# Opening of a two-block forward pass: two of the modulation loads get their own places, x and the small parameters change their turn, and ScalarE's copies change order

## The reference, cut to what matters

```python
def first_block(x, c, ada_w, ada_b, ...):
    cond = jax.nn.silu(c)
    for l in range(DEPTH):                                 # DEPTH = 2
        mod = (cond @ ada_w[l] + ada_b[l])[:, None, :]     # 1024 -> 6 * 1024
        sh_m, sc_m, g_m, sh_f, sc_f, g_f = jnp.split(mod, 6, axis=-1)
        h = x * (1.0 + sc_m) + sh_m
        y = even_mixer(h, ...) if l % 2 == 0 else odd_mixer(h, ...)
        x = layer_norm(DN_ALPHA * x + (1.0 + g_m) * y, ...)
        h = x * (1.0 + sc_f) + sh_f
        y = conv_ffn(h, ...)
        x = layer_norm(DN_ALPHA * x + (1.0 + g_f) * y, ...)
    return x
```

## Time and profile before

| | us |
|---|---|
| median of 3 runs (lowest, highest) | 1171.13 (1169.72, 1172.15) |
| the profiled execution, its own time | 1172.54 |
| its span from the first to the last instruction | 1170.7 |
| granted TensorE clock over the span | 0.989 |
| TensorE busy | 1120.4 |
| GpSimd busy | 832.1 |
| ScalarE busy | 590.6 |
| VectorE busy | 538.4 |

### The profile page before, as it was taken

How to read it: one execution, slowest core, us unless ns; L and a number is a source line. 1 busy time by engine, 2 the same in 40 slices (tenths; PEclk the granted TensorE clock), 3 DMA queues, 4 the chain that set the end, 5 groups by cost and what they waited for, 6 DMA issues and landing times.

```text
span 1170.7 us, 21670 instructions
## 1 busy us (share of the span) xinstructions
PE 1120.4 (96%) x8115; PEld 1026.8 (88%) x8115; DVE 538.4 (46%) x1120; ACT 590.6 (50%) x894; POOL 832.1 (71%) x297
## 2 busy tenths in 40 slices
PE   5899999999999989999999989999999999999997
PEld 2799898999998978899999878999999988999996
DVE  4668877865567675683232551342211333111112
ACT  0455535454544564455454445465876543545444
POOL 3567569988786545898878647556566776988884
PEclk9999999999999999899999999999999999999999
DMA  9987798999986536697566326344444544666562
GB/s 344 318 269 203 247 296 270 339 332 321 300 294 210 143 110 202 182 297 215 182 185 191 110 71 180 109 144 144 139 117 158 183 151 139 208 186 190 184 181 88
DMA packets 253484, 238.03 MB, mean 203 GB/s; under 512 B 18075, under 2 KB 216528, under 8 KB 253424
## 3 DMA queue, kind: packets, MB, share of 16 engines
q1 hardware_dynamic: 235104, 198.70, 55.4%
q10 hardware_dynamic: 17712, 38.28, 9.1%
q0 software_dynamic: 608, 0.22, 0.1%
HBM read 236.12 MB, written 1.05 MB: 203 GB/s over the span
## 4 chain that ended last, share of the span: by engine, by line
PE 68%; DMA 8%; POOL 7%; DVE 6%; ACT 6%; issue 3%; SPq 1%; ACTq 0%; POOLq 0%; DVEq 0%
PE bank L1287 17%; PE bank L1288 16%; PE bank L1289 16%; POOL unit_lo L733 6%; ACT unit_hi L849 3%; PE bank L1321 2%; PE bank L1312 2%; PE bank L1313 2%; DMA raw<-in_ffn_w_up 2%; DMA raw<-in_ev_w_in 2%; DMA ada<-in_ada_w 1%; PE bank L1425 1%; DVE x L2044 1%; PE bank L1528 1%; DMA accg<-in_ada_w 1%
## 5 line engine op out<-in xcount | busy, mean ns | idle before, releaser
L733 POOL TENSOR_TENSOR unit_lo<-raw,unit_hi 128x2048 fp32r<-128x2048 f32 (+5 forms) x87 | 343.7, 3955 | 216.8 <-ACT unit_hi L849 215.8
L1287 PE MATMUL bank<-h_hi,unit_hi 128*128 128x256 f32 x1152 | 327.0, 284 | 0.0
L1288 PE MATMUL bank<-h_lo,unit_hi 128*128 128x256 f32 x1152 | 325.9, 283 | 0.0
L1289 PE MATMUL bank<-h_hi,unit_lo 128*128 128x256 f32 x1152 | 325.9, 283 | 0.0
L784 POOL TENSOR_TENSOR unit_lo<-raw,unit_hi 128x2048 fp32r<-128x2048 f32 (+1 forms) x70 | 257.1, 3672 | 77.3 <-ACT unit_hi L998 65.6
L1287 PEld LDWEIGHTS bank<-h_hi,unit_hi 128*128 128x128 f32 x1152 | 220.7, 192 | 5.3 <-issue 2.5
L1288 PEld LDWEIGHTS bank<-h_lo,unit_hi 128*128 128x128 f32 x1152 | 220.7, 192 | 2.5
L1289 PEld LDWEIGHTS bank<-h_hi,unit_lo 128*128 128x128 f32 x1152 | 220.7, 192 | 0.0
L849 ACT ACTIVATE unit_hi<-raw 128x2048 fp32r<-128x2048 f32 (+5 forms) x97 | 161.2, 1663 | 101.5 <-PE bank L1289 30.3
L787 POOL TENSOR_TENSOR down<-raw_down,down 128x1024 fp32r<-128x1024 f32 x70 | 176.1, 2516 | 0.0
L2177 DVE SCALAR_TENSOR_TENSOR work<-bank,cols,work 128x254 f32<-128x254 f32 (+1 forms) x176 | 72.6, 474 | 131.7 <-ACT work L985 131.7
(11 more groups left out here) (363 smaller groups left out, 2173.3 us busy)
## 6 DMA issues: line engine op xcount, KB each, us to landing
raw<-in_ffn_w_up SPq DMA_DIRECT2D x86, 512.0 KB, 5.2
raw<-in_w_in SPq DMA_DIRECT2D x60, 512.0 KB, 4.7
raw_down<-in_ffn_w_down SPq DMA_DIRECT2D x44, 512.0 KB, 5.4
ada<-in_ada_w ACTq DMA_DIRECT2D x16, 1024.0 KB, 6.9
raw<-in_w_up SPq DMA_DIRECT2D x64, 256.0 KB, 3.0
raw_down<-in_w_down SPq DMA_DIRECT2D x32, 512.0 KB, 3.5
raw<-in_ev_w_in SPq DMA_DIRECT2D x28, 512.0 KB, 5.3
att<-in_ada_w ACTq DMA_DIRECT2D x14, 1024.0 KB, 7.7
```

What stands on the lines that cost most here:

```text
L733: nc.gpsimd.tensor_tensor(ul[g % 2][:, w], raw_home(g)[:, w], uh[g % 2][:, w].bitcast(F32), ALU.subtract).then_inc(lo_up, 1)
L1287: nc.tensor.matmul(o, sh, mh, start=first, stop=False)
L1288: nc.tensor.matmul(o, sh, ml, start=False, stop=False)
L1289: return nc.tensor.matmul(o, sl, mh, start=False, stop=last)
```

## The change

Four things change, all in the opening.

Half 3 of the late modulation (e = 2) gets a place of its own, columns 1024 to 3071 of `work`, and half 4 (e = 3) the two tiles `raw_down0` and `raw_down1`, in two DMAs of half the size. Each load has its own semaphore, and `load_mod` waits for nothing any more. TensorE's `mod_half(3)` waits for the second part before its third product.

The load of x stands behind all four modulation loads of each kind. On TensorE the transposes of x stand behind the last column products.

The transposes of the small parameters stand between the second and the third half product.

On ScalarE the high half of unit 0 stands behind the first `high` of h; it stood between the two row copies.

```diff
--- before.py
+++ after.py
@@ -401,7 +401,7 @@
         raw_in = [sem(f"raw_in{i}") for i in range(5)]
         rawd_in = [sem(f"rawd_in{i}") for i in range(2)]
         ada_in = [sem(f"ada_in{i}") for i in range(2)]
-        mod_in = [sem(f"mod_in{i}") for i in range(2)]
+        mod_in = [sem(f"mod_in{i}") for i in range(5)]
         hi_up, lo_up, hi_dn, lo_dn = sem("hi_up"), sem("lo_up"), sem("hi_dn"), sem("lo_dn")
         down_done = sem("down_done")
         c_in, stage_in, const_in, x_in, ln_in, pw_in, out_done = (sem(n) for n in (
@@ -434,6 +434,8 @@
         def raw_home(g):
 
             return hff if g == FFN_G0[0] else raw[g % 2]
+
+        late_mod = [work[:, D:D + CHUNKW], rawd[0][:, :], rawd[1][:, :]]
 
         def att_count(a, h):
 
@@ -617,11 +619,14 @@
 
             def load_mod(e):
 
-                if e >= 2:
-                    sp_.wait_ge(mod_done, e - 1)
-                s = e % 2
-                sp_.dma_start(ada[2 + s].rearrange("p (t n) -> p t n", t=KD // 2), half_of(0, MOD_PE[e // 2], s)
-                              ).then_inc(mod_in[s], 16)
+                src = half_of(0, MOD_PE[e // 2], e % 2)
+                if e < 3:
+                    home = ada[2 + e] if e < 2 else late_mod[0]
+                    sp_.dma_start(home.rearrange("p (t n) -> p t n", t=KD // 2), src).then_inc(mod_in[e], 16)
+                else:
+                    for i in range(2):
+                        sp_.dma_start(late_mod[1 + i].rearrange("p (t n) -> p t n", t=KD // 4), src[:, 2 * i:2 * i + 2, :]
+                                      ).then_inc(mod_in[3 + i], 16)
 
             def load_ada(a):
                 s = a % 2
@@ -635,8 +640,7 @@
             for a in range(MOD_START):
                 load_ada(a)
                 load_mod(a)
-                if a == MOD_START - 2:
-                    sp_.dma_start(x[:, :, :], W["x"][0].rearrange("(t p) n -> p t n", p=P)).then_inc(x_in, 16)
+            sp_.dma_start(x[:, :, :], W["x"][0].rearrange("(t p) n -> p t n", p=P)).then_inc(x_in, 16)
             for g in range(2):
                 load_unit(g)
             for a in SUM_FIRST:
@@ -874,6 +878,7 @@
 
                     whole(1)
                     high(0)
+                    hi_unit(0)
                     high(1)
                     whole(3)
                     high(2)
@@ -1037,8 +1042,6 @@
             b = full(act, "cond")
             nc.scalar.activation(cond, b[:, 0:KD], ACT.Exp, scale=-1.0).then_inc(cond_exp, 1)
             for i, j in enumerate(MOD_PE):
-                if i == 1:
-                    hi_unit(0)
                 act.wait_ge(mod_done, 2 * i + 2)
                 nc.scalar.activation(accg[0:1, AC * j:AC * (j + 1)], bank[4 + i][0:1, :], ACT.Copy).then_inc(mod_row, 1)
             h_high(0, ("modc", 0, 0), modT[:, 0, 8:16], modT[:, 0, 0:8])
@@ -1491,11 +1494,16 @@
             def mod_half(e):
 
                 i, s = e // 2, e % 2
-                pe.wait_ge(mod_in[s], 16 * (i + 1))
+                pe.wait_ge(mod_in[e], 16)
                 for q in range(KD // 2):
                     kt = KD // 2 * s + q
-                    mm = nc.tensor.matmul(bank[4 + i][0:1, :], cond[:, kt:kt + 1], ada[2 + s][:, AC * q:AC * (q + 1)],
-                                          start=kt == 0, stop=kt == KD - 1)
+                    if e < 3:
+                        w = (ada[2 + e] if e < 2 else late_mod[0])[:, AC * q:AC * (q + 1)]
+                    else:
+                        if q == 2:
+                            pe.wait_ge(mod_in[4], 16)
+                        w = late_mod[1 + q // 2][:, AC * (q % 2):AC * (q % 2 + 1)]
+                    mm = nc.tensor.matmul(bank[4 + i][0:1, :], cond[:, kt:kt + 1], w, start=kt == 0, stop=kt == KD - 1)
                 mm.then_inc(mod_done, 1)
 
             def late_rows(f):
@@ -1645,20 +1653,19 @@
             mm = nc.tensor.transpose(o[:, 0:KD], stage_c, ident[0:KD, 0:KD])
             done(mm, "cond")
             evacuated(pe, "cond")
-            for half in range(3):
+            for half in range(2):
                 mod_half(half)
-
             pe.wait_ge(stage_in, 16 * len(STAGED))
             o = begin("stage")
             for i, n in enumerate((PCOLS, P, P, 72)):
                 mm = nc.tensor.transpose(o[:, P * i:P * i + n], stage[i][0:n, :], ident[0:n, 0:n])
             done(mm, "stage")
-            pe.wait_ge(x_in, 16)
-            transpose_rows(0, x)
-
+            mod_half(2)
             mod_columns(0, (0,), js=[0, 1, 2, 3, 8, 9, 10, 11])
             mod_half(3)
             mod_columns(0, (0,), first=False, js=[4, 5, 6, 7, 12, 13, 14, 15])
+            pe.wait_ge(x_in, 16)
+            transpose_rows(0, x)
             first_units(0, G_QI[:1], low_last=True)
             unit_cols(G_QI[1], hh, hl)
```

## The result

The changed kernel takes 1178.99 us (median of 6 runs, 1176.86 to 1184.5), the kernel before 1171.27 us (6 runs, 1169.72 to 1172.15): **1.0063 times as long, interval 1.0043 to 1.0083**. The forecast was 1170.9 with 0.05 on slower; it was wrong in sign and size. The profiled execution of the changed kernel took 1177.72 us with a span of 1175.9, 5.2 us more than the span before.

A forecast was written before the change was run, and what follows sets the result against it. The prediction took the chain through GpSimd's low half of unit 1 to unit 3's low products as the bound; of 3.5 us sooner columns 0.2 us remained, off the median 1171.13, giving 1170.9 us, range 1169.3 to 1172.4.

The forecast's parts named there:

- the paragraph on GpSimd: GpSimd's low half of unit 0 starts 3.2 us later, using its idle; unit 1's ends at 46.8, gaining 0.2 to 0.3 us.
- The sum: Start of unit 3's low products moves from 59.99 to between 59.7 and 59.9; 0.2 us taken as the gain.
- Late small parameters: Rival: parameters landing at 25.0 delay half 3 to 25.6 and unit 3 by 3.8 us; 1174.9 us, chance 0.03.
- The late index keys: Rival: unit 2's reload of raw0 lands at 50.3, TensorE waits 2.2 us for its low half; 1172.3 us, chance 0.12.
- All four rivals: Gain comes through 1167.6 us, 0.03; unit 3 not bounding 1169.6, 0.13; index keys late 1172.3, 0.12; parameters late 1174.9, 0.03.
- The clock: TensorE's wait ahead of the first unit grows from 2.25 to 3.2 us; a later low-clock stretch costs nothing or 0.1 us.
- The bounding chain: Unit 1's high half, GpSimd's low half of it, then unit 3's load into raw1 and its halves set TensorE's 59.99.
- its early issue: Half 3's load goes out some 5 us sooner but still lands at 21.5, the DMA engines being full: nothing gained.
- The loss of cover for the transposes of x: On TensorE these 1.82 us now stand behind the last column products, 32.45 to 34.3, no longer covered by half 4's wait.
- TensorE's start behind the unit's half: TensorE waits for ScalarE's 1.91 us copy of unit 0 and starts the unit at 37.6, 0.6 us sooner than 38.23.
- the row copy's 0.85 us: The second column products' wait for ScalarE's row copy disappears: 0.85 us of the 3.5 us by which columns come sooner.
- this gain of 3.5 us in the modulation: Modulation columns ready at 32.9 instead of 36.42; only 0.2 to 0.3 us of it left after GpSimd's low halves.

The follow-up runs named there:

- e3: Kernel before with only ScalarE's order of the changed one (both row copies, then h, unit 0's high half behind its first h_hi copy): 1180.90 us, 1.0076.
- e7: Kernel before with h kept in its PSUM banks and nothing else changed: 1171.40 us, 0.9985 of the kernel before.
- e4: Changed kernel, all orders kept, with the first h in its PSUM bank, so the h_lo subtraction has one SBUF input: 1170.44 us, 1.0002 of the kernel before.
- e6: Changed kernel with h in its PSUM banks and unit 0's high half ahead of h on ScalarE: 1169.19 us, 0.9976 of the kernel before.

## Why the prediction was wrong

**The step that failed** is the paragraph on GpSimd: "Its low half of unit 0 ended at 39.00, with 3.43 us of idle behind it", followed by "The idle is gone, and GpSimd is now what is late". I took this idle for free room of GpSimd. It was the room in which VectorE did three of its four subtractions and the end of the first (39.00 to 41.43). With GpSimd's work in it the second and the third subtraction each waited for a low half (4.58 and 5.00 us), and the fourth waited behind the third. The sum had no term for `h_lo` at all: of VectorE's rows I read the modulation only, and wrote that ScalarE "has the same rest as before", as if h were ready when ScalarE was. The missing term is 4.5 us of idle and some 3.5 us of low clock around it, 8 us at unit 1. The 0.86 us of idle ahead of unit 3 swallowed a part, so 7 us went through where the forecast had a gain of 0.2.

**The rivals** didn't have it either. Two were on the slower side. Late small parameters did not come: they were turned at 20.52, ahead of the third half. The late index keys did not matter: TensorE reached their low products 8 us later anyway (61.26 against 53.20), without a wait. All four rivals asked when data comes and which wait ends last; none asked which two engines would now run at the same time that had not before.

**The clock.** The forecast put a longer low stretch at "Nothing, or 0.1 us", because idle of TensorE and its earlier start stood against it. The low stretch came around and behind the 4.18 us wait, on products that nothing paced, and its cost was not covered. Where low stretches fall also differs between executions where nothing was changed: half 4's products, with the same work of TensorE ahead of them, took 3.59 us in the earlier trace rows and 5.29 us in e3 and e7 (granted clock 1.00 over 29.5 to 33 us, against 0.64 and 0.67), which made h 0.7 to 0.8 us later there.

**What held.** The bounding chain was the right one. Without the lock, e4 gives 1.0002 with 0.9998 forecast; its interval of 0.2% to either side is far wider than the forecast's 0.2 us, so the trace says more. In e4 GpSimd's low halves end at 47.85, or 46.73 without the late start of 1.12 us in that execution, with 46.8 forecast. Unit 3's low products start at 60.37, so 59.25, with 59.7 to 59.9 forecast, and wait 0.36 us for GpSimd, not 1.5. The third half landed no sooner for its early issue (22.31 less the late start of 0.75 is 21.56, against 21.51). The loss of cover for the transposes of x, TensorE's start behind the unit's half (38.30, or 37.6 without that late start, as forecast) and the row copy's 0.85 us were sized rightly. The columns were ready at 33.76, or 33.0 without the late start, with 32.9 forecast. In e4, too, this gain of 3.5 us in the modulation brought nothing that the runs can tell: ScalarE's order kept it from the chain, as the prediction said.

**What stays open.** The changed kernel's own runs lie between 1176.86 and 1184.5. Between the two profiled executions single low stretches of the clock make differences of 1.7 us, so several of them could make such a spread; who goes first when both engines wait could, too. Neither was tried, and only one execution of the changed kernel was profiled.

## What to carry to other kernels

Idle time of an engine off the critical path is not free room: before moving work into it, list what every other engine does in that stretch, and ask whether the two share something. For VectorE and GpSimd that is their way into SBUF: a subtraction of 0.69 us that starts beside a low half of 4.6 us ends half a microsecond after that ends. Such a wait shows as a long instruction and not as idle time, so compare the shortest and the longest of equal instructions (before: 0.68 and 1.30 us). Where the two must overlap, keep one input of VectorE's instruction in PSUM; it costs no instruction here and took the loss of 0.6% away (e4), and with the unit's half ahead of h there was a gain of 0.2% (e6).

## What the runs showed of the hardware

The lock works both ways, and the engines take turns. In the changed kernel VectorE's second subtraction stood behind GpSimd's first low half, and the inputs of the third and the fourth were there by 40.72 (ScalarE's last `h_hi`); GpSimd's second low half was ready at 42.52. One subtraction went through (to 43.45), then GpSimd's low half, and only then the next subtraction. GpSimd's two low halves took 9.49 us there and 9.18 where VectorE read from PSUM. The same pair collides later in the kernel before, beside the change, in the layer norm's product or sum with a row (VectorE, line 2044; alone it takes 1.21 us at its shortest):

```profile
199.28 2.68 DVE L2044 TENSOR_TENSOR x<-x,att 128x1024 f32<-128x1024 f32 x1
...
196.27 4.60 POOL L784 TENSOR_TENSOR unit_lo<-raw,unit_hi 128x2048 fp32r<-128x2048 f32 x1 [2.46 <-ACT unit_hi L849]
200.83 3.40 POOL L787 TENSOR_TENSOR down<-raw_down,down 128x1024 fp32r<-128x1024 f32 x1
```

VectorE stands from 199.28 to GpSimd's end at 200.87 and is done at 201.96. GpSimd's next subtraction, on average 2.52 us in this kernel, takes 3.40 us, as if it stood behind VectorE in its turn (from 201.96 to its end at 204.23 are 2.27 us). No run tests this place.
